# Small vectors on ScalarE's queue, x ahead of the weights, the context's norm and transposes behind two projections

## What is computed

```python
mx = split(silu(c) @ w_ada + b_ada, 6)          # modulation of x
mc = split(silu(c_ctx) @ w_ada + b_ada, 6)      # modulation of the context
hx = _modulate(_rms_norm(x, g_pre_mix), mx[0], mx[1])
hc = _modulate(_rms_norm(ctx, g_pre_mix), mc[0], mc[1])
z = h @ w_in + b_in        # for hx and for hc; q, k, v, o, gates, conv inputs
```

## Time and profile before

| | us |
|---|---|
| median of 3 runs | 1755.04 |
| lowest and highest | 1752.9, 1756.14 |
| span of the profiled execution | 1752.8 |
| PE busy | 1413.3 (81%) |
| DVE busy | 386.8 (22%) |
| ACT busy | 261.3 (15%) |
| POOL busy | 96.6 (6%) |
| DMA | 515.38 MB, mean 294 GB/s |

### The profile page before, as it was taken

The page is one execution under the profiler, slowest core; times in us unless marked ns, Lnnn a source line. Parts: engine busy times, 40 slices in busy tenths (PEclk is TensorE's granted clock), DMA queues, the critical chain, the costliest instruction groups (busy, mean ns, idle before and its releaser), DMA issues.

```text
span 1752.8 us, 19020 instructions
## 1 busy us (share of the span) xinstructions
PE 1413.3 (81%) x7683; PEld 667.6 (38%) x7683; DVE 386.8 (22%) x918; ACT 261.3 (15%) x420; POOL 96.6 (6%) x128
## 2 busy tenths in 40 slices
PE   4988688669999999999998599897566666566655
PEld 2636244334444444444444374443321222122211
DVE  1212887531111111111111313322410000000002
ACT  2002012171111111111111201010600000000001
POOL 1002960000000000000000000000000000000000
PEclk9999777889999999999999899999686887788877
DMA  9367574418999999999992362225189999999994
GB/s 376 145 236 276 220 306 161 197 48 354 370 367 374 360 374 358 364 371 355 378 356 119 133 245 101 96 96 233 55 352 421 421 421 422 422 422 422 422 421 189
DMA packets 86535, 515.38 MB, mean 294 GB/s; under 512 B 7760, under 2 KB 11192, under 8 KB 36440
## 3 DMA queue, kind: packets, MB, share of 16 engines
q1 hardware_dynamic: 84744, 509.24, 72.6%
q0 software_dynamic: 1520, 5.39, 0.9%
q10 hardware_dynamic: 224, 0.09, 0.0%
HBM read 513.63 MB, written 1.06 MB: 294 GB/s over the span
## 4 chain that ended last, share of the span: by engine, by line
PE 63%; DMA 21%; DVE 8%; ACT 4%; issue 2%; SPq 1%; DVEq 0%; ACTq 0%
PE PS L1135 15%; DMA W<-in_w_expert_down 10%; DMA W<-in_w_expert_up 9%; PE PS L1160 9%; PE PS L1118 7%; PE PS L1105 6%; PE PS L883 5%; PE PS L1298 3%; ACT scr L722 3%; PE PS L836 2%; PE PS L1258 2%; PE PS L1040 2%; PE PS L1356 2%; PE PS L1341 2%; PE PS L1268 2%
## 5 line engine op out<-in xcount | busy, mean ns | idle before, releaser
L1135 PE MATMUL PS<-W,scr 128*64 128x512 f32 (+1 forms) x2048 | 405.3, 731 | 126.0 <-DMA W<-in_w_expert_up 63.0
L1135 PEld LDWEIGHTS PS<-W,scr 128*64 128x64 f32 (+1 forms) x2048 | 114.6, 144 | 408.6 <-issue 259.4
L1160 PE MATMUL PS<-W,scr 128*64 128x512 f32 (+1 forms) x1024 | 186.8, 646 | 35.1 <-DMA W<-in_w_expert_down 33.5
L1761 DVE TENSOR_TENSOR scr<-scr,PS 128x256 f32<-128x256 f32 (+1 forms) x40 | 27.7, 693 | 691.5 <-PE PS L1135 386.5
L1118 PE MATMUL PS<-scr 128*128 128x512 f32 x336 | 155.4, 605 | 4.9 <-ACT scr L744 2.6
L1105 PE MATMUL PS<-scr 128*128 128x128 bf16 x2016 | 123.2, 222 | 23.5 <-ACT scr L722 23.5
L1105 PEld LDWEIGHTS PS<-scr 128*128 128x128 bf16 x2016 | 119.7, 100 | 26.7 <-issue 26.2
L1160 PEld LDWEIGHTS PS<-W,scr 128*64 128x64 f32 (+1 forms) x1024 | 51.0, 131 | 139.8 <-issue 93.1
L733 ACT COPY scr<-PS 128x512 f32<-128x512 f32 x80 | 46.9, 586 | 356.1 <-PE PS L1105 356.1
L1118 PEld LDWEIGHTS PS<-scr 128*128 128x128 f32 x336 | 60.4, 189 | 100.5 <-issue 96.5
L744 ACT COPY scr<-PS 128x512 f32<-128x512 f32 x80 | 42.9, 589 | 223.4 <-PE PS L1160 223.4
(11 more groups left out here) (395 smaller groups left out, 1214.6 us busy)
## 6 DMA issues: line engine op xcount, KB each, us to landing
W<-in_we_gate SPq DMA_DIRECT2D x66, 1024.0 KB, 6.8
W<-in_we_up SPq DMA_DIRECT2D x66, 1024.0 KB, 8.9
W<-in_we_down SPq DMA_DIRECT2D x66, 1024.0 KB, 7.2
W<-in_w_expert_gate SPq DMA_DIRECT2D x64, 1024.0 KB, 18.5
W<-in_w_expert_up SPq DMA_DIRECT2D x64, 1024.0 KB, 19.1
W<-in_w_expert_down SPq DMA_DIRECT2D x64, 1024.0 KB, 19.1
W<-in_w_ada SPq DMA_DIRECT2D x12, 4096.0 KB, 13.9
W<-in_w_in SPq DMA_DIRECT2D x6, 4096.0 KB, 16.9
```

The lines of the kernel that those rows point to most:

```text
L1135: m = mm(dst if L == 2 else dst.rearrange("s (c n) -> s c n", c=2), hTe[:, k, j * cap:(j + 1) * cap], view[:, j, kk, :] if L == 2 else vie ...
L1160: m = mm(PS[6 + h][j * cap:(j + 1) * cap, :], aT[:, c, j * cap:(j + 1) * cap], view[:, j, cc, h * 512:(h + 1) * 512], start=(c == 0), stop ...
```

## The change

x is issued first of all by SP. The nine small vectors that SP issued are issued by ACT, behind its own seven and ahead of the two tables. ctx is issued behind in_qkv. On PE the context's transposes (`turned(1, ctxt)`) stand behind `project(0)` and `project(1)`. DVE normalises ctx behind the eight instructions that make hT, and prepares the bias rows behind its copies of q and k. ACT squares ctx behind ada1; since hT is being filled by then, the squares (which nobody reads) go to the tile osig.

```diff
@@ SP @@
             for n, i in AT.items():
-                if i == 1:
+                if i == 0:
                     sp.dma_start(x[:], A["x"][0].rearrange("(b p) d -> p b d", p=P)).then_inc(S["x_loaded"], 16)
-                    vec(0, C_CONVB, A["conv_b"][0], 4)
-                    vec(0, C_LNG, A["conv_ln_g"][0], 4)
-                    vec(0, C_LNB, A["conv_ln_b"][0], 4)
-                    vec(0, C_POOLS, A["pool_scale_2"][0], 4)
-                    vec(0, C_BQK, A["b_in"][0][0:512], 4)
-                    vec(0, C_BCONV, A["b_in"][0][1552:2576], 8)
-                    vec(1, 0, A["b_ada"][0], 48)
-                    vec(1, 48, A["b_ada_2"][0], 48)
-                    sp.dma_start(vecs[0:TAPS * 4, 2, :], A["conv_w"][0].rearrange("t (c p) -> (t c) p", p=P)).then_inc(S["vec_loaded"], 16)
-                if i == 2:
+                if i == 3:
                     sp.dma_start(ctxt, A["ctx"][0].rearrange("(b p) d -> p b d", p=P)).then_inc(S["ctx_loaded"], 16)
-                if i == 3:
                     row(rowb, A["b_in"][0][256:1552])
@@ ACT @@
             vec(0, C_N2, A["norm2_g_2"][0], 8)
+            vec(0, C_CONVB, A["conv_b"][0], 4)
...
+            vec(1, 48, A["b_ada_2"][0], 48)
+            act.dma_start(vecs[0:TAPS * 4, 2, :], A["conv_w"][0].rearrange("t (c p) -> (t c) p", p=P)).then_inc(S["vec_loaded"], 16)
             act.dma_start(relb, A["rel_bias_2"]).then_inc(S["rel_loaded"], 16)
...
-            for n, (src, loaded) in enumerate(((x, "x_loaded"), (ctxt, "ctx_loaded"))):
-                act.wait_ge(S[loaded], 16)
+            def mean_square(n, src):
                 for b in range(NB):
-                    step(a.activation(hT_words[:, b * D:(b + 1) * D], src[:, b, :], ACT.Square,
+                    step(a.activation(osig_words, src[:, b, :], ACT.Square,
                                       accum_out=st[:, 2 * n + b:2 * n + b + 1]), S["norm_sq"])
...
-                if n == 0:
-                    ada("ada0")
-
+
+            act.wait_ge(S["x_loaded"], 16)
+            mean_square(0, x)
+            ada("ada0")
             ada("ada1")
+            act.wait_ge(S["ctx_loaded"], 16)
+            mean_square(1, ctxt)
@@ PE @@
-            ada("ada0")
-            for n, src in enumerate((xn, ctxt)):
-                if n:
-                    ada("ada1")
-                    pe.wait_ge(S["ada_ready"], ada_done[2])
+            def turned(n, src):
                 pe.wait_ge(S["xnorm_ready"], n + 1)
...
+            ada("ada0")
+            turned(0, xn)
+            ada("ada1")
 
             pe.wait_ge(S["h_ready"], KD)
...
             project(1, [(m * T, T, feat(w_qkv, 256 + m * P), alltoks(hT)) for m in range(2)])
+            pe.wait_ge(S["ada_ready"], ada_done[2])
+            turned(1, ctxt)
             pe.wait_ge(S["hTc_ready"], KD)
@@ DVE @@
-            for n, src, dst in ((0, x, xn), (1, ctxt, ctxt)):
+            def normalised(n, src, dst):
                 dve.wait_ge(S["norm_sq"], 2 * n + 2)
...
+            normalised(0, x, xn)
...
-            dve.wait_ge(S["row_loaded"], 112)
-            step(v.tensor_scalar(rowb[:, 0:256], rowb[:, 0:256], DK ** -0.5, None, ALU.mult))
-            step(v.tensor_tensor(small[:, 344:360], rowb[:, 1280:1296], small[:, 344:360], ALU.add))
+            normalised(1, ctxt, ctxt)
...
+            dve.wait_ge(S["row_loaded"], 112)
+            step(v.tensor_scalar(rowb[:, 0:256], rowb[:, 0:256], DK ** -0.5, None, ALU.mult))
+            step(v.tensor_tensor(small[:, 344:360], rowb[:, 1280:1296], small[:, 344:360], ALU.add))
```

More of the change, by code:

```diff
@@ L184, in two_block_network @@
         osig = cv(NB, 512)
+        osig_words = osig.rearrange("p b n -> p (b n)")
         upad = cv(4, ROWS, ROW + 2 * HALO)
@@ L362, in _ @@
         def _(sp):
-            def vec(tile, at, ap, n):
-                sp.dma_start(vecs[at:at + n, tile, :], ap.rearrange("(k p) -> k p", p=P)).then_inc(S["vec_loaded"], 16)
             def row(dst, ap):
@@ L611, in _ @@
             vec(0, C_N2, A["norm2_g_2"][0], 8)
+            vec(0, C_CONVB, A["conv_b"][0], 4)
+            vec(0, C_LNG, A["conv_ln_g"][0], 4)
+            vec(0, C_LNB, A["conv_ln_b"][0], 4)
+            vec(0, C_POOLS, A["pool_scale_2"][0], 4)
+            vec(0, C_BQK, A["b_in"][0][0:512], 4)
+            vec(0, C_BCONV, A["b_in"][0][1552:2576], 8)
+            vec(1, 0, A["b_ada"][0], 48)
+            vec(1, 48, A["b_ada_2"][0], 48)
+            act.dma_start(vecs[0:TAPS * 4, 2, :], A["conv_w"][0].rearrange("t (c p) -> (t c) p", p=P)).then_inc(S["vec_loaded"], 16)
             act.dma_start(relb, A["rel_bias_2"]).then_inc(S["rel_loaded"], 16)
```

## The result

The changed kernel took 1761.98 us (median of 6 runs, 1758.35 to 1769.7) against 1754.97 us of the kernel before (median of 6, 1750.05 to 1756.14): a ratio of 1.0057, with an interval of 1.0034 to 1.0080. It is slower, by 7.0 us if the medians are subtracted and by 10 us if the ratio is taken. The profiled execution is the fastest of its six: 1758.35 us, span 1756.5, which is 3.7 us above the span before.

What follows compares the result with a forecast made beforehand. Up to 49.34 us, vector arrival and a chain of small steps bind, not weights; the context's work is hidden. -0.5 + 4.4 + 0.2 + 1.7 = +5.8 us gave 1760.8 us, range 1754 to 1765.

Steps and rivals of the forecast that it cites:

- Part 1, the vectors: Program start: vectors on ACT's queue let bucket land at 19.0 us and start L825 there instead of 19.46, -0.5 us.
- rival 3: Vector loads at the start: SP's full queue holds ACT's transfers up, about +14 us, 1769 us; chance 0.06.
- Part 2, x first and ctx late: Loads up to the projections: weights and ctx still land before they are needed, cost 0.
- Part 3, the hole: Ahead of project(2): PE makes 16 transposes, then waits for ACT's eight instructions, +4.4 us (4.1 to 5.0).
- bit quicker at full clock: First four context transposes, ahead of ACT's instructions: slightly faster at full clock, so 4.4 us instead of 4.5.
- Part 4, the clock at the projections' start: Start of the projections: clock is low before and after, longer PE idling adds only +0.2 us.
- Part 4, the clock behind the hole: From project(2) on: clock falls, 3.4 us at half clock, +1.7 us (0 to 2.3).
- rival 1: Behind the context's transposes and wait: clock stays up, +4.1 us, 1759.1 us, bounds +2.8 to +4.8; chance 0.25.
- Rival 2: Program start: tables there at 13.1 us, -6.3 us pays for the hole, 1755.0 us; bucket before 13.2 decides; chance 0.17.
- The signs of the profile after: Expected: first projection 0 to 1 us ahead of 49.34, hole 4.1 to 5.0, project(2) at 68 to 70, clock 0.50 behind.

Runs made afterwards that it cites:

- e2: Kernel before with x first and the nine vectors on ACT's queue, context as before: 1753.23 us, ratio 1.0007.
- e6: Changed kernel plus ten unread 128x512 products where PE waits for hT ahead of project(0): 1765.12 us, ratio 1.0078.
- e5: Changed kernel with the context's transposes between project(0) and project(1) instead of behind both: 1755.9 us, ratio 1.0021.
- e4: Changed kernel with conv_w's 124 rows loaded as two transfers of 112 and 12 rows: 1756.24 us, ratio 1.0038.
- e3: Changed kernel with the vectors back on SP's queue, context still late and turned behind project(1): 1759.68 us, ratio 1.0053.
- e1: Changed kernel again, no edit, for a second trace and more runs: 1761.09 us, ratio 1.0056.
- e8: Kernel before again, no edit, for another trace: 1754.35 us profiled, span 1752.6 us.
- e9: Kernel before once more, no edit, for a further trace: 1758.5 us profiled, span 1756.8 us.
- e7: Kernel before with split conv_w and both b_ada vectors on SP ahead of ada0, six others on ACT: 1750.66 us, ratio 0.9993; timed again, 1748.34 us, 0.9978.

## Why the prediction was right, point by point

The forecast was +5.8 us, slower by more than 0.2%. The times give +7.0 (medians) or +10 (ratio), the two traces of the changed kernel +3.7 and +5.9. The side and the place were right; some terms were mis-sized, in part against each other. That the number came so near is luck in part: a gain of 3.8 us that was in no term stands in both traces of the changed kernel.

- **Part 1, the vectors: -0.5 forecast, +1.4 and +0.9 measured** (product with the table at 20.88 and 20.34 instead of 19.46; 19.91 in e2). All five traces with the changed loads (e6 at 20.80 and e5 at 20.15 are the others) lie above the 18.2 to 19.5 that the prediction gave. The reading of rows 5 held: e4 fits four engines for conv_w. The mis-sized step is 52 packets times 0.18 us on top of 9.6 us: it put bucket's landing at 19.0, and it came at 20.84. The DMA views of 6:7, 14:15 and 17:18 us of the profile after (q1 is SP's queue, q10 ACT's; packets, MB, share):

```profile
q1 hardware_dynamic: 101, 0.41, 100.4%
q10 hardware_dynamic: 8, 0.00, 1.1%
```

```profile
q1 hardware_dynamic: 93, 0.38, 98.9%
q10 hardware_dynamic: 22, 0.01, 4.0%
```

```profile
q10 hardware_dynamic: 20, 0.01, 3.3%
```

  22 and 20 packets per us on four engines are 5.5 and 5 per engine, a cadence of 0.18 to 0.20 us: near the 0.18 taken. But in 6:7 only 8 packets of ACT's went through, where rows 4 had 42. Most of an us passed with nearly nothing of ACT's queue; what held it there is open, and so is whether rival 3's mechanism has a part in it.
- **Part 2, x first and ctx late: 0 forecast.** Right: no wait for x, ctx, ada0's or ada1's weights shows in the chain after, and e2, which has x first, is level. In e3, with ctx late, the projections start at 49.49 us, beside 49.34.
- **Part 3, the hole: +4.4 forecast, 4.58 measured** (63.79 to 68.37; 4.57 to 4.59 in e1, e3, e4 and e6). The rows of the kernel before (3.75 us of ACT, the first four transposes ahead of them) gave it nearly. Only the "bit quicker at full clock" wasn't there: ACT starts 0.77 us behind the first transpose at either clock. e3 has the hole without the vectors' part, e5 takes 2.8 us of it away.
- **Part 4, the clock at the projections' start: +0.2 forecast, +1.4 measured** (64 products in 16.78 us, 16.60 in e1, instead of 15.36). This term was mis-sized. I argued that the clock is low there before and after; it is, but in the profile after the half clock lasts for 5.8 us of products instead of 3.0. e6 puts the whole cost of it at 2.96 us. The transposes that have gone from there don't explain it by themselves, as these traces show (us, from start to start for the products):

| | before | e2 | e3 | after |
|---|---|---|---|---|
| transposes of ctx ahead of the projections | yes | yes | no | no |
| ada0's 32 products | 6.05 | 6.46 | 6.03 | 5.58 |
| clock at 0.50 in the ada chain | 31.8 to 38.6 | 33.1 to 36.5 | 32.1 to 38.9 | never |
| clock at 0.50 at the projections | 45.5 to 52.3 | 43.5 to 53.7 | 45.7 to 52.5 | 42.5 to 52.9 |
| the 64 products | 15.36 | 16.21 | 15.39 | 16.78 |

  e3 has no transposes there and its products are as fast as before; e2 has them and its products are slower. What decides when the clock falls and how long it stays low is open.
- **Part 4, the clock behind the hole: +1.7 forecast**, with a stay at full clock as rival 1. It fell in e1, e3 and e4 (8.86 us each time instead of 7.17) and stayed up in the first trace of the changed kernel and in e6, where the hole is the same. The size was right, the event is not certain. What the Trainium skill ("TensorE: Matmul & The Clock Gate", section "Part 4: PE-mode transpose") says of transposes, which the prediction weighed, decides it in neither direction here: with the same transposes and the same wait both happened.
- **Not forecast: -3.8 us** between ada0's start and the first projection, where the clock stayed at 1.00. It is there in after, e1, e4 and e5 (21.7 to 22.2 us from ada0's start to the first projection), and not in before, e2, e3, e8 and e9 (25.0 to 26.2). e6 has it too, up to its added products: 15.2 us from ada0's start to ada1's sums, as in after (15.4), where before has 19.2. The five have both the loads and the late context of the change; either part alone (e2, e3) doesn't bring it. One thing divides all fourteen traces in the same way: the five took 5.2 to 5.8 us for ada0's 32 products, the nine without the gain, those of e7's kernel among them, 6.0 to 6.6 us. Up to there PE's stream is the same in all of them. Why they differ is open. Together with the row before, the stretch from ada0's start to the end of project(1) became 2.4 us shorter in the first trace and 2.9 to 3.0 in e1 and e4, where the prediction had +0.2. If this gain were missing in most untraced runs, the sums would be 3.7 + 3.8 = 7.5 for the first trace, 5.9 + 4.2 = 10.1 for e1, 0.0 + 3.6 = 3.6 for e5, and 1.5 + 4.2 = 5.7 for e4, beside 10.0, 9.8, 3.7 and 6.7 by the ratios. That is near for three of them, but it is argued and not shown; for e7's kernel, whose traces show more gain than its times, it explains nothing.
- **Rival 2** was excluded by its own mark (13.2 us; measured 20.3 to 20.9). e4 and e7 reached 15.75 and 12.02 with other transfers; in e7 the early start was then worth less in time than in the traces. **Rival 3** would have been at 28 and was not.
- **Two slips in the sums, which decide nothing.** By the bounds of the range, rival 1's upper end is 0 + 5.0 + 0.8 = 5.8 and not 4.8. Rival 3's terms add up to 8.5 + 4.4 + 0.2 + 1.7 = 14.8, not 14.
- **The signs of the profile after.** In the first trace project(2)'s start (68.37) and the hole (4.58) were as given, and the clock of 1.00 behind it was the sign of rival 1; e1's project(2) started at 67.31, ahead of the 68 given. The first projection came 2.3 us ahead of 49.34 and not 0 to 1, by the clock in the ada chain.

What is not settled: what keeps the clock up in the ada chain, and why 7 us at the start of e7's kernel come out as 1 to 4 in its times. The delays of e3 and e6 (4.8 and 6.0 us at project(2)) came out as more, 9.3 and 13.7 by the ratios; that is not explained either.

## What to carry to other kernels

Work that is hidden because another engine sets the time beside it is free there and may cost elsewhere: here 16 transposes and eight copies cost nothing ahead of the first projection (e3, without them, is 0.1 us faster from ada0 to there), 1.75 us between two projections whose products cover the copies, and 4.6 us directly ahead of the consumer. Don't lay a change of the clock on the nearest edit before a trace with that edit alone shows it: here the missing transposes looked like the reason for slower products, but e3 lacks them too and its products are as fast as before. And look at the row count of a small transfer before its bytes: 124 rows in one piece held the start up for some 5 us longer than 112 and 12.

## What the hardware showed that I had not expected

- The clock is not a fixed function of the program: the same kernel fell to 0.50 behind the hole in one trace and not in the other, and the kernel before fell to it between 131.5 and 138.3 us in e9 and not in e8. Such a fall costs up to 3.5 us, as much as the first trace's whole shift.
- Ten products of 512 columns did not keep the clock up. It fell 0.4 us after they began, and the work that was meant to hold the clock up ran itself at half clock for 3.4 us.
- A short packet of ACT's queue beside SP's stream of long ones took a slot of 0.18 to 0.20 us on its engine (22 and 20 packets per us, on four engines), and ACT's queue went almost unserved for an us (8 packets from 6 to 7 us, where before had 42).
